# Routing of a two-layer mixture-of-experts kernel: positions without totals, one-hots tile by tile, pair tables moved into the first expert

## What is computed

```python
def route(hf, w_router, b_router):
    logits = (hf @ w_router).astype(jnp.float32) + b_router.astype(jnp.float32)
    probs = jax.nn.softmax(logits, axis=-1)
    grouped = probs.reshape(t, N_GROUPS, EXPERTS_PER_GROUP)
    group_score = lax.top_k(grouped, TOP_K)[0].sum(-1)
    sel_group = jnp.argmax(group_score, axis=-1)
    in_group = jnp.take_along_axis(grouped, sel_group[:, None, None], axis=1)[:, 0]
    top_p, top_local = lax.top_k(in_group, TOP_K)
    expert_idx = sel_group[:, None] * EXPERTS_PER_GROUP + top_local
    weights = top_p / jnp.sum(top_p, axis=-1, keepdims=True)
    return expert_idx, weights
```

## Time and profile before

| what | value |
|---|---|
| median of 3 runs | 1478.76 us (1477.57 to 1478.95) |
| the profiled execution | 1479.38 us |
| its span | 1477.8 us |
| TensorE busy | 1442.4 us (98%) |
| VectorE busy | 1133.3 us (77%) |
| ScalarE busy | 773.2 us (52%) |
| GpSimd busy | 143.4 us (10%) |
| mean granted TensorE clock | 0.996 |

### The profile page before, as it was taken

One profiled execution on the slowest core, in us unless ns is written; L12 is line 12 of the kernel. 1 busy time (PEld: TensorE's weight loads), 2 busy tenths in 40 slices (PEclk: granted clock), 3 DMA queues, 4 the chain that ended last, 5 costly groups with the idle time before them and its releaser, 6 DMA issues.

```text
span 1477.8 us, 18814 instructions
## 1 busy us (share of the span) xinstructions
PE 1442.4 (98%) x6824; PEld 1155.0 (78%) x6824; DVE 1133.3 (77%) x1532; ACT 773.2 (52%) x1102; POOL 143.4 (10%) x139
## 2 busy tenths in 40 slices
PE   6999999999999999999989999999999999999997
PEld 3788887778877778888858888878888787888884
DVE  5774677455669999999987657854345899999998
ACT  3333433223256888888733344342233488888883
POOL 0000001000002211111100000100000112211010
PEclk9999999999999999999999999999999999999999
DMA  8856466455557999999956543642254879999995
GB/s 346 306 185 195 160 212 199 144 186 159 199 205 249 381 390 390 383 392 378 358 220 206 189 140 115 195 145 88 86 171 147 287 283 393 394 388 393 378 378 207
DMA packets 107413, 377.49 MB, mean 255 GB/s; under 512 B 16521, under 2 KB 16713, under 8 KB 106548
## 3 DMA queue, kind: packets, MB, share of 16 engines
q1 hardware_dynamic: 90864, 331.39, 62.0%
q0 software_dynamic: 15200, 40.62, 7.7%
q10 hardware_dynamic: 1252, 4.22, 0.8%
HBM read 361.32 MB, written 34.64 MB: 268 GB/s over the span
## 4 chain that ended last, share of the span: by engine, by line
PE 83%; DVE 11%; DMA 2%; ACT 1%; issue 1%; DVEq 1%; ACTq 0%; SPq 0%
PE ps L1759 25%; PE ps L1761 24%; PE ps L1760 24%; DVE w_lo L1510 3%; DVE w_lo_more L1510 3%; DMA raw<-w 2%; PE ps L1844 2%; PE ps L2018 1%; PE ps L1913 1%; PE ps L2067 1%; PE ps L1917 1%; DVE xgT_lo L1499 1%; DVE y_out L1533 1%; DVE w_lo L1007 1%; PE ps L1948 0%
## 5 line engine op out<-in xcount | busy, mean ns | idle before, releaser
L1007 DVE TENSOR_TENSOR w_lo<-raw,w_hi 128x1024 fp32r<-128x1024 f32 x132 | 161.3, 1224 | 213.9 <-ACT w_hi L651 212.6
L651 ACT ACTIVATE w_hi<-raw 128x1024 fp32r<-128x1024 f32 x132 | 139.1, 1058 | 334.2 <-PE ps L1761 332.5
L1510 DVE TENSOR_TENSOR w_lo<-raw,w_hi 128x1024 fp32r<-128x1024 f32 x188 | 224.2, 1216 | 3.9 <-ACT w_hi L836 3.0
L1759 PE MATMUL ps<-w_hi,hT_lo 128*128 128x512 f32 x512 | 206.6, 404 | 4.1 <-DVE hT_lo L1110 4.1
L1510 DVE TENSOR_TENSOR w_lo_more<-raw,w_hi_more 128x1024 fp32r<-128x1024 f32 x172 | 205.2, 1216 | 2.4 <-ACT w_hi_more L836 1.3
L836 ACT ACTIVATE w_hi<-raw 128x1024 fp32r<-128x1024 f32 x188 | 193.5, 1058 | 24.5 <-DMA raw<-w 15.1
L1761 PE MATMUL ps<-w_hi,hT_hi 128*128 128x512 f32 x512 | 200.4, 391 | 0.0
L1760 PE MATMUL ps<-w_lo,hT_hi 128*128 128x512 f32 x512 | 200.0, 391 | 0.0
L836 ACT ACTIVATE w_hi_more<-raw 128x1024 fp32r<-128x1024 f32 x172 | 177.0, 1057 | 25.2 <-DMA raw<-w 15.7
L1759 PE MATMUL ps<-hT_hi,w_lo 128*128 128x512 f32 x320 | 130.5, 408 | 0.0
L1761 PE MATMUL ps<-hT_hi,w_hi 128*128 128x512 f32 x320 | 125.0, 391 | 0.0
(11 more groups left out here) (285 smaller groups left out, 2629.1 us busy)
## 6 DMA issues: line engine op xcount, KB each, us to landing
raw<-w SPq DMA_DIRECT2D x590, 512.0 KB, 7.2
h_rows<-h POOLq DMA_DIRECT2D x8, 1024.0 KB, 5.2
ahead<-w SPq DMA_DIRECT2D x4, 2048.0 KB, 11.2
x_state<-x POOLq DMA_DIRECT2D x2, 2048.0 KB, 10.1
y_rows<-x_in ACTq DMA_DIRECT2D x4, 1024.0 KB, 12.5
x<-x_state POOLq DMA_DIRECT2D x4, 1024.0 KB, 6.1
pair_early<-y_rows SPq DMA_DIRECT2D x4, 1024.0 KB, 6.4
x<-x_in SPq DMA_DIRECT2D x4, 512.0 KB, 12.8
```

Source lines behind the costliest of these rows:

```text
L651: act.activation(w_hi[:, q % W_SLOTS], stream_piece(l, q, r), ACT.Copy).then_inc(w_hi_ready, 1)
L1007: v.tensor_tensor(w_lo[:, q % W_SLOTS], stream_piece(l, q, r), w_hi[:, q % W_SLOTS], ALU.subtract).then_inc(raw_used, 1)
L1510: v.tensor_tensor(ring_lo(e * EXP + n), expert_piece(e, n), ring_hi(e * EXP + n), ALU.subtract).then_inc(raw_used, 1)
L1759: pe.matmul(dst, a_lo, b_hi, start=start, stop=False)
```

## The change

- VectorE computes `two` later and drops `best` from the place ahead of `chosen`; `chosen_f` comes right behind `chosen`.
- The positions and the totals are two semaphore steps. `pos` is copied in two parts, the totals later and from bank 6.
- Each `hot0` has a step of its own, and `first_rows_selected` waits tile by tile.
- The last tile's rows are made in halves of 512 columns, the first scaling ahead of the last logits; `j = 0` of the selection waits only for the first half (`h2_half`).
- The pair shares, `pair_weights` and `overflow_count` move behind `hidT(1)` and two pieces of the first expert.
- `hot` is made after the four `w_lo` pieces; `row_ids` follows `gate_up(3)` instead of `gate_up(1)`, and `idx` is written inside the first expert.
- `keep_busy(9)` becomes `keep_busy(2)`.

```diff
@@ -442,6 +442,7 @@
         chosen_ready = sem("chosen_ready")
         pos_ready = sem("pos_ready")
         hot0_ready = sem("hot0_ready")
+        h2_half = sem("h2_half")
         hot_ready = sem("hot_ready")
         idx_sum = sem("idx_sum")
         idx_ready = sem("idx_ready")
@@ -1356,6 +1357,7 @@
                 for t in range(NT - 1):
                     token_logits(t)
                 inverse_deviation(l * 8 + 4, NT - 1)
+                last_h2_scaled(0)
                 v.wait_ge(logits_ready, l * 2 + 2)
                 token_logits(NT - 1)
                 v.drain()
@@ -1366,61 +1368,74 @@
                 beaten_by(beats[:].rearrange("p (s n) -> p s n", n=16), lg4)
                 v.tensor_reduce(ranks[:], beats[:].rearrange("p (a b) -> p a b", b=4), AX, ALU.add)
                 v.drain()
-                v.tensor_scalar(two[:], ranks[:], 1.0, None, ALU.is_le)
-                v.tensor_scalar(best[:], ranks[:], 0.0, None, ALU.is_equal)
                 v.wait_ge(exp_done, l + 1)
                 v.scalar_tensor_tensor(rt[:, 0:64], ranks[:], 1.0, probs[:], ALU.is_le, ALU.mult)
                 v.drain()
                 v.tensor_reduce(s4[:], rt[:, 0:64].rearrange("p (s e) -> p s e", e=4), AX, ALU.add)
-                v.tensor_scalar(second[:], ranks[:], 1.0, None, ALU.is_equal)
+                v.tensor_scalar(two[:], ranks[:], 1.0, None, ALU.is_le)
                 v.drain()
                 beaten_by(group_beats[:].rearrange("p (t n) -> p t n", n=16), s43)
                 v.tensor_reduce(group_rank[:], group_beats[:].rearrange("p (a b) -> p a b", b=4), AX, ALU.add)
                 v.drain()
                 best_group = group_rank[:].unsqueeze(2).broadcast_to([P, NT * NG, 4])
                 in_best_group(chosen[:], two).then_inc(chosen_ready, 1)
+                in_best_group(chosen_f[:], two)
+                v.tensor_scalar(best[:], ranks[:], 0.0, None, ALU.is_equal)
+                v.tensor_scalar(second[:], ranks[:], 1.0, None, ALU.is_equal)
+                v.wait_ge(pos_ready, l * 2 + 1)
+                v.tensor_copy(pos[:, 0:64], ps[:, 7, 0:64])
+                v.drain()
+                for t in range(NT):
+                    v.tensor_scalar(hot0[:, t], k("iota"), pos[:, NE * t:NE * t + 1], chosen_f[:, NE * t:NE * t + 1],
+                                    ALU.is_equal, ALU.mult).then_inc(hot0_ready, 1)
+                last_h2_shifted(0).then_inc(h2_half, 1)
+                last_h2_scaled(1)
                 in_best_group(hots[:, 0:64], best)
                 in_best_group(hots[:, 64:128], second)
-                in_best_group(chosen_f[:], two)
-                v.drain()
-                v.tensor_tensor(rt[:].rearrange("p (j n) -> p j n", j=2), hots[:].rearrange("p (j n) -> p j n", j=2),
-                                probs[:].unsqueeze(1).broadcast_to([P, 2, NE * NT]), ALU.mult)
-                v.wait_ge(pos_ready, l + 1)
-                v.tensor_copy(pos[:], ps[:, 7, 0:80])
-                v.drain()
-                for t in range(NT):
-                    one = v.tensor_scalar(hot0[:, t], k("iota"), pos[:, NE * t:NE * t + 1], chosen_f[:, NE * t:NE * t + 1],
-                                          ALU.is_equal, ALU.mult)
-                one.then_inc(hot0_ready, 1)
-                v.scalar_tensor_tensor(h2[NT - 1][:], x[:, NT - 1], x_rs[:, NT - 1:NT], scale_row[:], ALU.mult, ALU.mult)
-                v.tensor_reduce(top[:], rt[:].rearrange("p (s e) -> p s e", e=NE), AX, ALU.add)
-                v.drain()
-                v.tensor_tensor(h2[NT - 1][:], h2[NT - 1][:], shift_row[:], ALU.add).then_inc(h_ready, 1)
-                v.tensor_tensor(r1[:], top[:, 0:4], top[:, 4:8], ALU.add)
-                v.drain()
-                v.reciprocal(r1[:], r1[:])
-                v.drain()
-                v.tensor_tensor(wts[:, 0:4], top[:, 0:4], r1[:], ALU.mult)
-                v.tensor_tensor(wts[:, 4:8], top[:, 4:8], r1[:], ALU.mult)
+                v.drain()
+                last_h2_shifted(1).then_inc(h_ready, 1)
+                lo(l, MIX, RAW_MIX)
+                both_chosen(posk, pos[:, 0:64])
+                v.wait_ge(pos_ready, l * 2 + 2)
+                v.tensor_copy(pos[:, 64:80], ps[:, 6, 480:496])
                 v.tensor_tensor(hotid[:].rearrange("p (s e) -> p s e", e=NE), hots[:].rearrange("p (s e) -> p s e", e=NE),
                                 k("slotid").unsqueeze(2).broadcast_to([P, 2 * NT, NE]), ALU.mult)
-
-
-                both_chosen(posk, pos[:, 0:64])
-                lo(l, MIX, RAW_MIX)
+                gathered_lo(l * NE, 0, [0])
+                lo(l, MIX + 1, RAW_MIX + 1)
+                lo(l, MIX + 2, RAW_MIX + 2)
+                gathered_lo(l * NE, 0, [1])
+                lo(l, MIX + 3, RAW_MIX + 3)
                 for j in range(2):
                     for t in range(NT):
                         one = v.tensor_scalar(hot[:, j, t], k("iota"), posk[:, 4 * j + t:4 * j + t + 1], None, ALU.is_equal)
                 one.then_inc(hot_ready, 1)
-                pair_weights()
-                gathered_lo(l * NE, 0, [0])
-                lo(l, MIX + 1, RAW_MIX + 1)
-                overflow_count()
-                gathered_lo(l * NE, 0, [1])
-                for q in range(2, W_SLOTS):
-                    lo(l, MIX + q, RAW_MIX + q)
+
+            def last_h2_scaled(half):
+                cols = slice(512 * half, 512 * half + 512)
+                v.scalar_tensor_tensor(h2[NT - 1][:, cols], x[:, NT - 1, cols], x_rs[:, NT - 1:NT], scale_row[:, cols],
+                                       ALU.mult, ALU.mult)
+
+            def last_h2_shifted(half):
+                cols = slice(512 * half, 512 * half + 512)
+                return v.tensor_tensor(h2[NT - 1][:, cols], h2[NT - 1][:, cols], shift_row[:, cols], ALU.add)
+
+            def row_numbers(l):
                 v.wait_ge(idx_sum, l + 1)
                 v.tensor_scalar(idx[:], ps[:, 6, 496:512], -1.0, None, ALU.add).then_inc(idx_ready, 1)
+
+            def pair_shares():
+
+                v.tensor_tensor(rt[:].rearrange("p (j n) -> p j n", j=2), hots[:].rearrange("p (j n) -> p j n", j=2),
+                                probs[:].unsqueeze(1).broadcast_to([P, 2, NE * NT]), ALU.mult)
+                v.drain()
+                v.tensor_reduce(top[:], rt[:].rearrange("p (s e) -> p s e", e=NE), AX, ALU.add)
+                v.drain()
+                v.tensor_tensor(r1[:], top[:, 0:4], top[:, 4:8], ALU.add)
+                v.drain()
+                v.reciprocal(r1[:], r1[:])
+                v.drain()
+                v.tensor_tensor(wts[:, 0:4], top[:, 0:4], r1[:], ALU.mult)
+                v.tensor_tensor(wts[:, 4:8], top[:, 4:8], r1[:], ALU.mult)
             def pair_weights():
@@ -1565,6 +1580,8 @@
                 else:
                     lo_e(next(pieces))
                     lo_e(next(pieces))
+                    if e == 0:
+                        row_numbers(l)
                     if e:
                         rows_out(e - 1)
                     hidden(0)
@@ -1578,6 +1595,10 @@
                     hidT(1)
                     lo_e(next(pieces))
                     lo_e(next(pieces))
+                    if e == 0:
+                        pair_shares()
+                        pair_weights()
+                        overflow_count()
                     gathered_lo(E + 1, 1 - odd, [0])
                     lo_e(next(pieces))
                     gathered_lo(E + 1, 1 - odd, [1])
@@ -1956,10 +1977,14 @@
             def first_rows_selected(l):
-                pe.wait_ge(hot0_ready, l + 1)
                 for j in range(2):
                     for t in range(NT):
-                        pe.wait_ge(h_ready, l * 8 + (4 + t + 1))
+                        if j == 0:
+                            pe.wait_ge(hot0_ready, l * NT + (t + 1))
+                        if j == 0 and t == NT - 1:
+                            pe.wait_ge(h2_half, l + 1)
+                        else:
+                            pe.wait_ge(h_ready, l * 8 + (4 + t + 1))
                         for i in range(4):
                             c = (4 * j + i) * P
                             one = pe.matmul(ps[:, 4 + j, i * P:(i + 1) * P], h2[t][:, c:c + P], hot0[:, t],
@@ -2069,7 +2094,7 @@
                 for n in range(6):
                     gate_up(n)
-                    if e == 0 and n == 1:
+                    if e == 0 and n == 3:
                         row_ids(l)
                 hidden_transposes(0)
                 gate_up(6)
@@ -2180,11 +2205,12 @@
                 pe.wait_ge(chosen_ready, l + 1)
                 pe.matmul(ps[:, 7, 0:NE * NT], before_r[:], chosen[:], start=True, stop=False)
                 for s in range(1, NT):
-                    pe.matmul(ps[:, 7, NE * s:NE * NT], ones_r[:], chosen[:, 0:NE * (NT - s)], start=False, stop=s == NT - 1)
```

(6 more changed lines are left out.)

16 lines of the change are left out of this document (8 added, 8 removed).

## The result

| | kernel before | kernel after |
| --- | --- | --- |
| median, us | 1477.96 (1477.00 to 1478.95, 9 runs) | 1482.06 (1478.88 to 1488.57, 9 runs) |
| ratio to before | | 1.0037, 95% interval 1.0026 to 1.0047 |
| profiled execution, its span, us | 1479.38, 1477.8 | 1481.58, 1480.0 |
| TensorE busy, share of the span | 98% | 97% |
| TensorE's wait for `xgT_lo`, all waits, us | 2.1 | 5.6 |

The change makes the kernel 4.1 us slower, 0.37%, and it scatters: nine executions of before lie within 2 us, nine of the change within 10. The mean granted clock that each execution lists goes with its time: 0.999 at 1478.88 us, 0.996 or 0.997 at 1480.65 to 1482.06, 0.993 to 0.995 at 1483.61 to 1488.57.

A forecast was written before the change was run, and what follows sets the result against it. VectorE was taken as the bound from routing to about the sixth expert, DMA close behind. Two layers at +0.35 us gave +0.7, less 0.2 for a pause: +0.5 on 1478.76, 1479.3 us; range 1475.8 to 1482.2 us.

The forecast's parts named there:

- rival (c): Routing or first expert, both layers: TensorE's clock falls after cut fillers and new waits; +2.7 us, 1482.0 us, chance 0.07.
- Up to `chosen`: End of logits to `chosen`: `two` and `best` leave their places, so the next product starts 0.21 us earlier.
- The selection: Routing: positions without totals and one-hots tile by tile let the selection start at 1159.2 instead of 1160.86.
- The first product: First expert's start: `gate_up(0)` begins at 1166.5 instead of 1169.05, 2.6 us earlier, and its 0.88 us wait goes.
- `hidT(1)`: First expert, VectorE: this row starts at 1181.7 instead of 1184.99, the whole lead of 3.3 us.
- What takes it back: Behind `hidT(1)`: the moved block's 3.89 us make the second expert's `gathered_lo` 0.6 us later; a layer loses 0.35 us.
- VectorE without idle time between the block and the first `y_out`: First expert's end: the lag stays because VectorE has no idle time; idle time there would prove the sum wrong.
- the gather: First expert: GpSimd's first gather issues 1.4 us earlier; TensorE waits one or two microseconds for it, at cost 0.
- the expert window: Profile row between routing and about the sixth expert: granted clock 1.00 despite small waits, taken as evidence against a clock fall.
- The sum of VectorE's rows: Up to the second expert: VectorE's rows put `gathered_lo` 0.6 us later, net 0.35 us lost a layer.

The follow-up runs named there:

- the fillers in the pause: The changed kernel with ten filler matmuls on TensorE between the first and second expert: 1479.36 us, ratio 1.0007 to the kernel before.
- The later wait on the change alone: The changed kernel with only VectorE's wait for gate_row's landing moved from ahead of the experts into the second expert: 1482.37 us, ratio 1.0031.
- the block in pieces: The changed kernel with the moved block split over three places, in the routing and the first expert: 1475.19 us, ratio 0.9979 to before.

## Why the prediction was wrong

The forecast was 1479.3 us, no change that could be told; the kernel became 4.1 us slower, clear of noise. 1482.06 us lies just inside the stated range, at the end that was stretched to take in rival (c).

**What held**, counted from `chosen` in the second layer (1157.49 before, 1158.89 after):

- *Up to `chosen`*: from the last logits 3.87 us instead of 4.04, so 0.17 us earlier; forecast 0.21.
- *The selection*: 1.75 us behind `chosen` instead of 3.37, 1.62 us earlier; forecast 1.66.
- *The first product*: 8.82 instead of 11.56, 2.7 us earlier; forecast 2.6.
- *`hidT(1)`*: 24.24 instead of 27.50, 3.26 us earlier; forecast 3.3.
- *What takes it back*: the block 4.27 us with its pause, 3.84 without; forecast 3.89. The low halves 31.12 instead of 30.11, 1.0 us later; in the first layer 30.65 instead of 30.48, 0.2 later. The forecast's 0.6 stands in the middle. The pause without a releaser of the earlier trace rows is gone from the pair shares of the first layer, which gives 0.6 - 0.43 there; another has come up inside the block in the second, which gives 0.6 + 0.43. The forecast had only the first.
- VectorE without idle time between the block and the first `y_out`: so it was in the second layer. In the first it idles 0.59 us for a `w_hi` piece at 473.95, behind the fall of the clock.

**What failed.** The step is the half sentence "TensorE finishes the first expert about three microseconds early and waits more than one for this row", and with it rival (c). The wait is 2.70 and 2.91 us. The numbers for it were there, in the paragraph on the gather: TensorE is there at 1181.8, needs 3.6 us more, and VectorE holds it to 1188.9, which makes 3.5 us of waits. Measured in the second layer are 0.72 us for the gather and 2.91 for the row, 3.6 together. Only by giving the gather one to two of them does the pause come out near two. I had it as a consequence to look for and gave it no price. Its price is the clock: 3.3 us of the median, by the fillers in the pause, where the sum had nothing.

Rival (c) had the fall of the clock and, at 1482.0 us, the time, but the time in part by luck: it put the fall ahead of `hidT(1)`, at 1.35 us in both layers, while the falls came behind it, at the second expert, with 1.7 us of clock each and in one layer of two in both profiles of the change. Its chance of 0.07 rested on "the longest new pause is near two microseconds" and on the cut fillers, and both were wrong: putting the fillers back made it worse. The rule of the Trainium skill weighed there ("TensorE: Matmul & The Clock Gate", section "Loop structure matters more than you think") is borne out for long waits between matmuls (3.36 to 3.86 us, five falls of five) and not for the cut, behind which the clock stays at 1.00 in the change up to the second expert; the expert window at 1.00, which I set against it, has no wait of this length in it.

A second step missed a wait: *the gather*. VectorE's wait for `gate_row`, 0.30 us in the first layer and 0.90 in the second, was hidden before by VectorE's own lateness, and the routing's saving brought it to light. So in the second layer the first gather came 17.48 us behind `chosen` instead of 18.01, 0.5 us earlier and not 1.4 (in the first 17.07 instead of 18.37), and TensorE waited 0.57 and 0.72 us for it. The later wait on the change alone shows that this cost nothing in the end: without it TensorE only waits longer for the low halves.

The sum of VectorE's rows was off by little. `y_out` of the second expert comes 1.6 and 1.0 us later than before, counted from `chosen`, where 0.6 was forecast (+0.35 a layer with what is gained ahead of `chosen`). In the first layer the clock is in that. The second, with no fall, gives the better number: 0.6 and the pause of 0.43. Over both layers the fillers in the pause leave 1.2 us, against +0.5 forecast, and the interval of that run (-0.3 to +2.4 us) holds both.

## What to carry to other kernels

When a producer is the bound and its consumer gains a lead, a lump of small work right ahead of the row that the consumer needs next turns the whole lead into one pause. Work out that pause as lead plus delay, and ask what TensorE's clock makes of it, before calling the lump's cost its length less the lead. The same 3.9 us cut into three pieces, each of which holds up TensorE by 0.8 us at most, turned the loss into a gain here (0.9979 of before against 1.0037).

## What was not expected of the hardware

- A single wait of TensorE of 2.5 to 2.9 us in a stretch otherwise busy brought the granted clock from 2.4 to 1.2 GHz in one layer and not in the other of the same execution, and the longer of the two was not always the one; waits from 3.36 us on did in each of five. The waits of up to 1.6 us ahead of an expert never did in these profiles.
- Ten matmuls whose result is not used, in a pause of that length, made the kernel 3.3 us faster in the median, and 4.4 us where the pause was longer.
- VectorE's pause of 0.40 to 0.43 us with no releaser turns up in chains of small operations, between the routing and the second expert once a layer at most, and at the same instruction in both executions of the change that were profiled: at `posk` in the first layer and at `ovn` in the second. It is at the reciprocal in the first layer of the kernel before, and at the count's reduction in the second layer with the block in pieces. What makes it stays open.
- That no lump hides in the experts 8 to 12 was read from the `y_out` rows; why the spare microseconds of TensorE there don't take it up was not tried apart.
